# A hybrid decoder step: the exponentials of the prompt attention put ahead of the copy of transposed probabilities on ScalarE

## The reference

```python
def masked_softmax(s, mask):
    s = jnp.where(mask, s.astype(jnp.float32), NEG)
    return jnp.where(mask, jax.nn.softmax(s, axis=-1), 0.0)
...
    s = jnp.einsum('bqghd,bqgksd->bqghks', q, k_g) * scale
...
    o_slc = jnp.einsum('bqghks,bqgksd->bqghd', p.reshape(shp).astype(v_g.dtype), v_g)
    s = jnp.einsum('bqghd,bwgd->bqghw', q, kw) * scale
...
    p = masked_softmax(s, wmask[None, :, None, None, :])
    o_win = jnp.einsum('bqghw,bwgd->bqghd', p.astype(vw.dtype), vw)
    g = jax.nn.sigmoid(gates)
    return g[..., 0:1] * o_cmp + g[..., 1:2] * o_slc + g[..., 2:3] * o_win
```

## Time and profile before

| | us |
|---|---|
| median of 3 runs | 1360.94 |
| profiled execution, whole | 1362.09 |
| its span | 1360.3 |
| PE busy (share of the span) | 1251.7 (92%) |
| DVE busy | 830.0 (61%) |
| ACT busy | 306.2 (23%) |
| POOL busy | 356.2 (26%) |

### The profile page before, as it was taken

How to read it: one execution, slowest core, us unless ns; L and a number is a source line. 1 busy time by engine, 2 the same in 40 slices (tenths; PEclk the granted TensorE clock), 3 DMA queues, 4 the chain that set the end, 5 groups by cost and what they waited for, 6 DMA issues and landing times.

```text
span 1360.3 us, 20576 instructions
## 1 busy us (share of the span) xinstructions
PE 1251.7 (92%) x7761; PEld 1017.7 (75%) x7761; DVE 830.0 (61%) x1370; ACT 306.2 (23%) x831; POOL 356.2 (26%) x422
## 2 busy tenths in 40 slices
PE   6999899999999668999999999986999999999995
PEld 5878776668887445556788888775888888888885
DVE  7779332227888477877766554757565465466445
ACT  3463311120010355655410011032000000000012
POOL 5942324312220022322112111110111112513542
PEclk9899899899999889999999999996999999999998
DMA  9223445547667333435461322331122132131101
GB/s 261 57 96 120 147 105 169 165 137 263 244 247 247 103 94 109 146 112 164 166 235 64 108 64 108 140 105 35 62 93 93 63 111 75 62 124 63 63 1 63
DMA packets 122002, 166.15 MB, mean 122 GB/s; under 512 B 36448, under 2 KB 90400, under 8 KB 117552
## 3 DMA queue, kind: packets, MB, share of 16 engines
q1 hardware_dynamic: 103408, 104.72, 24.7%
q0 software_dynamic: 8080, 50.58, 10.4%
q10 hardware_dynamic: 10416, 9.54, 2.1%
HBM read 159.34 MB, written 13.84 MB: 127 GB/s over the span
## 4 chain that ended last, share of the span: by engine, by line
PE 82%; DVE 10%; ACT 3%; issue 3%; POOL 0%; DMA 0%; DVEq 0%; ACTq 0%; PEldq 0%
PE PS L2272 44%; PE PS L1865 12%; PE PS L2036 9%; PE PS L1842 4%; PE PS L2180 2%; PE PS L2148 2%; PE PS L1991 2%; PE PS L2210 1%; DVE small L1654 1%; DVE PS L1652 1%; PE PS L1974 1%; PE PS L2015 1%; DVE R L1672 1%; PE PS L2185 1%; ACT QO L970 1%
## 5 line engine op out<-in xcount | busy, mean ns | idle before, releaser
L1865 PE MATMUL PS<-hT,stream 128*128 128x260 f32 (+1 forms) x800 | 190.2, 399 | 7.2 <-ACT KVU L1056 4.1
L1865 PEld LDWEIGHTS PS<-hT,stream 128*128 128x128 f32 (+1 forms) x800 | 155.6, 197 | 39.8 <-issue 6.3
L2272 PE MATMUL PS<-R,stream 128*128 128x260 f32 x720 | 168.9, 383 | 2.5 <-PE PS L2272 2.5
L2272 PEld LDWEIGHTS PS<-R,stream 128*128 128x128 f32 x720 | 135.7, 190 | 25.8 <-issue 5.5
L2272 PE MATMUL PS<-R 128*128 128x260 f32 x576 | 132.4, 386 | 3.3 <-DVE R L1817 2.1
L2036 PE MATMUL PS<-R 128*128 128x256 f32 (+1 forms) x544 | 121.8, 383 | 5.2 <-DVE R L1495 2.4
L2272 PEld LDWEIGHTS PS<-R 128*128 128x128 f32 x576 | 110.4, 192 | 21.5 <-DVE R L1817 2.5
L2272 PE MATMUL PS<-R,QO 128*128 128x260 f32 x544 | 123.6, 383 | 1.4 <-DVE QO L1698 1.4
L1772 DVE TENSOR_TENSOR R<-PS,R 128x260 f32<-128x260 f32 x100 | 42.6, 426 | 127.7 <-PE PS L2272 126.9
L2036 PEld LDWEIGHTS PS<-R 128*128 128x128 f32 x544 | 102.1, 197 | 22.1 <-issue 6.1
L2272 PEld LDWEIGHTS PS<-R,QO 128*128 128x128 f32 x544 | 103.3, 190 | 17.6 <-DVE QO L1698 1.8
(11 more groups left out here) (420 smaller groups left out, 1931.9 us busy)
## 6 DMA issues: line engine op xcount, KB each, us to landing
stream<-in_cache_kv_slc SPq DMA_DIRECT2D x128, 128.0 KB, 2.1
stream<-in_w_mlp_up SPq DMA_DIRECT2D x8, 2048.0 KB, 8.0
stream<-in_w_mlp_down SPq DMA_DIRECT2D x8, 2048.0 KB, 7.5
stream<-in_w_in SPq DMA_DIRECT2D x4, 2048.0 KB, 11.2
stream<-in_state_kv_win SPq DMA_DIRECT2D x16, 512.0 KB, 5.3
stream<-in_w_in SPq DMA_DIRECT2D x8, 1024.0 KB, 19.7
out_kv_win_sample<-in_state_kv_win POOLq DMA_DIRECT2D x1, 8176.0 KB, 43.5
R<-in_cache_kv_slc SPq DMA_DIRECT2D x56, 128.0 KB
```

Source lines behind the costliest of these rows:

```text
L1865: ins = M(pair(u)[0:w, hf, 0:HALF], lhs[k], rhs[k][:, HALF * hf:HALF * hf + HALF], start=(k == 0), stop=(k == n - 1))
L2272: ins = M(product_of(w, i), lhs[:, k, :], rhs[:, k, :], start=(k == 0), stop=(k == nk - 1))
```

## The change

In the loop on ACT the exponentials of task n now stand ahead of the copy of task n-2. Since they write the buffer `PP[:, n % 2]` that the transposes of task n-2 read, they now wait for these transposes with `at_full` as well. Nothing else is changed. The line numbers behind the change shift by two at most: the exponentials are L1155 in the kernel after, the copy L1164, the output copy L1169.

```diff
@@ -1145,6 +1145,16 @@
             for n in range(NTK + 3):
+                if n < NTK:
+                    t = TASKS[n][0]
+                    act.wait_ge(as_max, n + 1)
+                    if n >= 2:
+                        act.wait_ge(at_full, n - 1)
+                    for i, x, j, c0 in softmaxes(n):
+                        k = 4 * (n % 2) + i
+                        ins = nc.scalar.activation(PP[:, n % 2, j, c0:c0 + P * (t + 1)], score_block(n, j, c0),
+                                                   ACT.Exp, bias=amx[:, k:k + 1], accum_out=asm[:, k:k + 1])
+                    ins.then_inc(as_exp, 1)
                 if 2 <= n <= NTK + 1:
                     m = n - 2
                     t, p, h, r, nx = TASKS[m]
@@ -1153,14 +1163,6 @@
                         act.wait_ge(ao_full, m - 1)
                     nc.scalar.activation(blocks(m, PTP[:, m % 2, 0, :], P * (t + 1)),
                                          blocks(m, PS[:, 5, :], P * (t + 1)), ACT.Copy).then_inc(at_a, 1)
-                if n < NTK:
-                    t = TASKS[n][0]
-                    act.wait_ge(as_max, n + 1)
-                    for i, x, j, c0 in softmaxes(n):
-                        k = 4 * (n % 2) + i
-                        ins = nc.scalar.activation(PP[:, n % 2, j, c0:c0 + P * (t + 1)], score_block(n, j, c0),
-                                                   ACT.Exp, bias=amx[:, k:k + 1], accum_out=asm[:, k:k + 1])
-                    ins.then_inc(as_exp, 1)
                 if n >= 3 and TASKS[n - 3][3] == 1:
                     act.wait_ge(ao_full, n - 2)
                     nx = TASKS[n - 3][4]
```

## The result

The changed kernel takes 1378.49 us (median of 4 runs, 1377.1 to 1379.44) against 1361.42 for the kernel before in the same session (4 runs): ratio 1.012, 95% interval 1.0107 to 1.0134, so 17.1 us slower, 14.6 to 18.2 by the interval. The forecast was 1376.5 with a range of 1370 to 1385. In all, 23 runs of the changed kernel are on record, from 1374.7 to 1380.17, with a median of 1377.92.

A forecast was written before the change was run, and what follows sets the result against it. TensorE, busy 157.06 of the loop's 167 us, was taken as nearly full; growth of 5.1 + 4.9 + 2.7 + 2.6 = 15.3 us took the profiled 1362.09 to 1377.4, less 1.15 for the median: 1376.5 us, range 1370 to 1385.

The forecast's parts named there:

- Nothing is gained: Attention loop, ACT: exp(n) waits for its maximum, so it could start only 0.0 to 0.1 us sooner; taken as 0.
- The chain of exponentials and copy: Growing loop steps: transposes, exponentials, copy, next transposes in series; 3.89 us against 3.16 at t = 3, +0.73.
- the term from copy to TensorE: Loop: from the end of ACT's copy to TensorE's next transposes, taken as 0.11 us, between 0.03 and 0.2.
- Every second step recovers: Loop: after a grown step the maximum is in time, so the next doesn't grow; 3.30 us at t = 3.
- The sum: Whole loop: 5.1 us at t = 3, 4.9 at t = 2, 2.7 at t = 1, 2.6 at t = 0, together 15.3.
- The unknown costs: Loop: second wait 0 to 2 us, copy to TensorE -2 to +2, output copy up to 4; waits taken as 0.
- The clock: Loop: TensorE's granted clock was 1.00 throughout, also in its thinnest piece; a low-clock stretch costs about 3.4 us per 10.
- Rival B: Loop: the granted clock falls in two stretches as at 300 us, +7, so 1383 us; chance 0.05.
- All outside 497 to 680 us keeps its length: Outside the attention loop: no part of the kernel changes its length.
- A (no recovery): Loop: steps between the growing ones grow too, except with a decode block; +7, so 1384 us; chance 0.09.
- C (hidden): Loop: the copy's lateness falls where TensorE has other work, steps unchanged, 1361 us; chance 0.05.
- D (faster): Loop, mainly t = 0: exp(n) starts 0.4 to 0.6 us earlier, -7, so 1354 us; chance 0.04.

The follow-up runs named there:

- e4: Changed kernel with three buffers for the probabilities, so the exponentials need no wait for the transposes of n-2: 1380.24 us, ratio 1.0121 to the kernel before.
- e3: Kernel before with ACT's copy of n-2 placed between two halves of the exponentials in every iteration: 1366.65 us, ratio 1.003.
- e2: Kernel before with the new ACT order in odd iterations only, the old order in even ones: 1364.91 us, ratio 1.0021.
- e12: Kernel before, old ACT order, with only the exponentials' added wait for the transposes of n-2: 1361.56 us (one run).
- e8: Kernel before with DVE's reciprocals moved ahead of the maxima, and one ACT instruction copying both banks at t = 0 and 1: 1358.1 us, ratio 0.9975.
- e5: Kernel before with the new ACT order for t = 2 and 3 only, the old one for t = 0 and 1: 1372.14 us, ratio 1.0071.
- e6: Kernel before with DVE's reciprocals of n-1 moved between the mask and the maxima of n: 1358.7 us, ratio 0.9977.
- e1: Kernel before with the new ACT order in even iterations only, the old order in odd ones: 1379.68 us, ratio 1.013.

## Why the prediction was right

*Nothing is gained.* In the long steps exp(n) starts 1.84 us after the transposes at t = 3, 1.58 at t = 2 and 2.11 at t = 1, before and after. Shown by the change's own trace; e4 adds that it isn't the new wait that holds it there. It is not so at the edges of a stretch: in steps 2, 4 and 16 the exponentials start 0.1, 0.1 and 0.4 us sooner, which the forecast took as nothing.

*The chain of exponentials and copy.* Right in kind, and within 0.06 us in size: 3.83 for 3.89 at t = 3, 3.25 for 3.31 at t = 2, 4.58 for 4.64 at t = 1, 3.40 for 3.46 at t = 0. The whole difference is the term from copy to TensorE, which the prediction took as 0.11 without a row for it: it is 0.05 (0.053 us before rounding) each time that the transposes wait for the copy. e3 shows that this chain is the cause: with the copy put half a group sooner the steps at t = 3 are back at 3.16.

*Every second step recovers.* Right: 3.32 us, for 3.30 before, and by the cause that the prediction gave, a maximum that comes in time because the step ahead was long. e2 is the test of it: with the step ahead short the odd steps grow as well.

*The sum.* 15.3 us were forecast for the loop. Even steps gave 14.0 (with the 0.06 over 22 steps, 1.3 less), odd steps outside steps 9 and 11 some 0.6. That is 14.7 us. At t = 0 the sum came out by luck: four times 0.64 was forecast after the pattern of step 6, and steps 2, 4, 6 and 8 grew by 0.6, 0.5, 0.6 and 1.0. The other 2.8 us of the 17.4 lie in steps 9 and 11, the two with the low clock.

*The unknown costs.* The second wait was 0 within 0.02 us (e12), and no row stood behind the 0.1 that it might have cost. The output copy cost nothing in the changed kernel, where no wait of TensorE's values for it is left; in e3 and e8 it does. TensorE's transposes wait 22.8 us for ACT's copy and not "some 15", since these waits took the place of the 9.1 us for DVE and GpSimd.

*The clock.* The forecast took 1.00 for the loop, since its thinnest stretch had it. That term failed. I judged by the busy share of ten microseconds and did not write down how long the single waits would be: by the rows 0.94 + 0.64 = 1.58 us at t = 0 (1.52 in step 6), and 2.06 in step 8, whose exponentials are already the longer ones of t = 1 and which I had taken as like the others. Rival B was therefore partly true: two stretches, but 2.8 us for both and not 7.
The rule that I cited from the Trainium skill, "TensorE: Matmul & The Clock Gate" (a second failure mode), had the outcome right: with more and longer pauses between groups of matmuls the low clock came, in two pieces. That the pauses bring it is not shown here. The pauses of 0.65 us at t = 2 and 3, of which there are many more, did not (e5), and e12 has a low-clock piece with no pause over 0.67 us in the 6 us ahead of it.

*Outside the loop.* "All outside 497 to 680 us keeps its length" did not hold: behind the loop the changed kernel is 1.69 us shorter in this profile, and 1.55 in the second one. The new order is not needed for that, since e12 in the old order has the same 697.5 us; the cause stays open. In this profile it hides more than half of the 2.8 us that the low clock cost in the loop. So that the measured time is only 2.0 us above the forecast is in part luck.

*Rivals.* A (no recovery) is out by the 3.32 us steps, C (hidden) by the time, D (faster) by the starts of the exponentials, which are unmoved in the long steps.

## What to carry to other kernels

An engine's idle time ahead of an instruction is worth nothing to the instruction behind it if that one has its own, later condition; compare the start of the second with the end of the first and with its own last releaser before exchanging them. Put first what another engine is about to wait for, even if it is the short instruction. In a loop with two steps in flight, follow the effect over two steps: a step that grew can pay for the next, and single changes need not add up.

## What the runs showed of the hardware that I had not expected

Scaling 512 columns on GpSimd (L640) took 1.04 us when DVE's own scaling of the other half, and then its copy, ran at the same time, and 0.77 when DVE took the maxima from PSUM meanwhile. From the instructions of that line, t = 3, the kernel before and then the one with early reciprocals (e6) (durations in ns, minimum, median, maximum):

```profile
L640 POOL TENSOR_SCALAR R<-R,small x13: 1039/1041/1043, 613.4 to 658.0; 128x512 f32<-128x512 f32 x13
```

```profile
L640 POOL TENSOR_SCALAR R<-R,small x12: 767/767/768, 611.7 to 652.5; 128x512 f32<-128x512 f32 x12
```

ACT's exponentials and DVE's copy run beside the slow ones too, but they are not needed: in the last task of the changed kernel only DVE's scaling does, with the end of one copy on ACT, and it is 1.04 again.

```profile
676.67 0.59 ACT L1164 ACTIVATE R<-PS 128x512 f32<-128x512 f32 x1
...
677.01 0.55 DVE L640 TENSOR_SCALAR R<-R,small 128x512 f32<-128x512 f32 x1
677.08 1.04 POOL L640 TENSOR_SCALAR R<-R,small 128x512 f32<-128x512 f32 x1 [0.65 <-DVE small L1661]
```

So 0.27 us are lost beside 0.48 us of DVE's scaling. That it is DVE's use of SBUF is my reading; no run here was made to test it.

The low-clock pieces in the loop came at the same two steps in both profiles of the changed kernel and in e1, and one of them costs 1.6 us (step 11, 5.17 with it and 3.54 without, in e4). Outside the loop the profile of e3 has one more such piece than that of the kernel before and is 1.75 us longer there. Whether such pieces are also most of the scatter between executions of one kernel is not shown: of the two kernels with two profiles, neither has its two apart by a whole piece behind the loop.
